# Weight panels beside the inverse and the chunk walk, loaded by transfers of 8 partitions

## What is computed

```python
def step(S, inp):
    r_t, d_t, k_t, v_t, kk_t, b_t = inp
    sa = jnp.einsum('bhvk,bhk->bhv', S, kk_t)
    S = S * d_t[:, :, None, :] - sa[..., None] * b_t[:, :, None, :] + v_t[..., None] * k_t[:, :, None, :]
    y = jnp.einsum('bhvk,bhk->bhv', S, r_t)
    return S, y
...
y = ((y - mean) * lax.rsqrt(var + GN_EPS)).reshape(B, T, D) * gn_w + gn_b
y = (y + bonus.reshape(B, T, D)) * jax.nn.silu(gp)
return y.astype(h.dtype) @ w_out
```

## The kernel before, in words

| panel | slot | what | used up by |
|---|---|---|---|
| 9, 10 | 1, 2 | the two g projections | PE, at about 122 and 145 us |
| 11 to 16 | 3, 0, 1, 2, 3, 0 | gate rows ("ada_rows") 2 to 7 | DVE, four quarters each |
| 17 | 1 | gate panel 8, direct | PE (`ada_direct`, L599), after the walk |
| 18, 19 | 2, 3 | wo_a, both halves | PE, after the walk |
| 20, 21 | 0, 1 | k1, both halves | PE |

## Time and profile before

### The profile page before, as it was taken

How to read it: one execution, slowest core, us unless ns; L and a number is a source line. 1 busy time by engine, 2 the same in 40 slices (tenths; PEclk the granted TensorE clock), 3 DMA queues, 4 the chain that set the end, 5 groups by cost and what they waited for, 6 DMA issues and landing times.

```text
span 1040.6 us, 19605 instructions
## 1 busy us (share of the span) xinstructions
PE 990.0 (95%) x8274; PEld 862.4 (83%) x8274; DVE 745.7 (72%) x1245; ACT 526.0 (51%) x798; POOL 36.5 (4%) x33
## 2 busy tenths in 40 slices
PE   5999999978999999999989999999999899999996
PEld 4888899977788888788857899999698788999995
DVE  5789989577889958646589666666587895664444
ACT  3258431316544686455466445454465855445441
POOL 0000044200000100000000000000000000000000
PEclk9999999989999999999999999999999999999999
DMA  9684410393456560564264478777656444486411
GB/s 366 229 317 162 162 44 4 112 400 143 162 218 232 198 243 26 218 243 162 81 243 162 172 294 291 296 293 266 224 189 230 172 162 162 180 295 253 169 75 41
DMA packets 56263, 205.36 MB, mean 197 GB/s; under 512 B 6376, under 2 KB 6376, under 8 KB 56176
## 3 DMA queue, kind: packets, MB, share of 16 engines
q1 hardware_dynamic: 55584, 202.50, 52.6%
q10 hardware_dynamic: 592, 1.61, 0.5%
HBM read 203.03 MB, written 1.05 MB: 196 GB/s over the span
## 4 chain that ended last, share of the span: by engine, by line
PE 85%; DVE 8%; ACT 3%; DMA 2%; issue 2%; SPq 0%; DVEq 0%; ACTq 0%
PE bank L454 21%; PE bank L455 20%; PE bank L456 20%; PE bank L764 5%; PE bank L403 4%; DVE slot_parts L2027 2%; PE bank L667 1%; DMA ring<-in_stream 1%; PE bank L561 1%; PE bank L906 1%; PE bank L745 1%; PE bank L640 1%; DMA pc<-in_params 1%; PE bank L629 1%; PE bank L536 1%
## 5 line engine op out<-in xcount | busy, mean ns | idle before, releaser
L454 PE MATMUL bank<-page_parts 128*128 128x512 f32 (+3 forms) x1222 | 428.5, 351 | 8.2 <-DVE page_parts L2309 2.1
L2027 DVE TENSOR_TENSOR slot_parts<-ring,page_parts 128x2048 fp32r<-128x2048 f32 (+2 forms) x117 | 261.5, 2252 | 59.4 <-ACT page_parts L1365 59.0
L456 PE MATMUL bank<-page_parts 128*128 128x512 f32 (+2 forms) x750 | 290.7, 388 | 0.0
L455 PE MATMUL bank<-slot_parts,page_parts 128*128 128x512 f32 (+2 forms) x750 | 290.7, 388 | 0.0
L454 PEld LDWEIGHTS bank<-page_parts 128*128 128x128 f32 x1222 | 231.8, 190 | 38.5 <-issue 3.6
L1365 ACT ACTIVATE page_parts<-ring 128x2048 fp32r<-128x2048 f32 (+2 forms) x121 | 224.8, 1883 | 58.0 <-DMA ring<-in_stream 28.0
L456 PEld LDWEIGHTS bank<-page_parts 128*128 128x128 f32 x750 | 141.2, 188 | 29.0
L455 PEld LDWEIGHTS bank<-slot_parts,page_parts 128*128 128x128 f32 x750 | 141.4, 189 | 26.4
L1443 ACT ACTIVATE arena<-bank 128x512 f32<-128x512 f32 (+2 forms) x134 | 74.2, 575 | 128.2 <-PE bank L456 66.9
L455 PE MATMUL bank<-page_parts 128*128 128x256 f32 x472 | 133.6, 283 | 0.0
L456 PE MATMUL bank<-page_parts,slot_parts 128*128 128x256 f32 x472 | 133.6, 283 | 0.0
(11 more groups left out here) (317 smaller groups left out, 1104.6 us busy)
## 6 DMA issues: line engine op xcount, KB each, us to landing
ring<-in_stream SPq DMA_DIRECT2D x380, 512.0 KB, 6.1
arena<-in_x SPq DMA_DIRECT2D x2, 512.0 KB, 4.2
arena<-in_gn ACTq DMA_DIRECT2D x2, 512.0 KB, 4.6
out<-arena SPq DMA_DIRECT2D x2, 512.0 KB, 2.6
cc<-in_consts SPq DMA_DIRECT2D x1, 835.5 KB, 6.5
small<-in_cond ACTq DMA_DIRECT2D x1, 512.0 KB, 7.0
pc<-in_params SPq DMA_DIRECT2D x1, 287.0 KB, 6.9
arena<-in_head_sel ACTq DMA_DIRECT2D x1, 32.0 KB
```

Source lines behind the costliest of these rows:

```text
L454: mm(out, a[0], b[0], start=start, stop=False)
L455: mm(out, a[0], b[1], start=False, stop=False)
L456: return mm(out, a[1], b[0], start=False, stop=stop)
L2027: tt(unit_parts(n)[1], lo, hi, ALU.subtract).then_inc(dv.step("w_lo"), 1)
```

## The change

The nine panels 11 to 19 are loaded in 16 transfers of 8 partitions x 4096 columns instead of 4 transfers of 128 x 1024. What a slot's semaphore must reach is now summed over the panels that went through the slot (`loaded`), 256 for such a panel, 64 for the others. The wait ahead of ("ada_rows", 5) is gone. DVE does four quarters of gate rows at the end of `beside(4)`, and four instead of six before each of the first two copies of S. The waits at lines 384, 592, 1360, 1373 and 1998 all take the new count.

```diff
-PIECES = 4
+PIECES, ROWS = 4, 8
...
+        beside_short_products = [("ada_rows", n) for n in range(2, 8)] + [("ada", 8), ("wo_a", 0), ("wo_a", 1)]
+
+        def narrow(i):
+
+            return order[i][0] in beside_short_products
+
+        def loaded(i):
+
+            return 16 * sum(P // ROWS if narrow(j) else PIECES for j in range(i % SLOTS, i + 1, SLOTS))
...
-                pe.wait_ge(sem(f"slot_loaded{i % SLOTS}"), 16 * PIECES * (i // SLOTS + 1))
+                pe.wait_ge(sem(f"slot_loaded{i % SLOTS}"), loaded(i))
...
                     sp.wait_ge(*order[i - SLOTS][1])
-                if name == ("ada_rows", 5):
-                    sp.wait_ge(*finished(("X", 5, 3)))
+                if narrow(i):
+                    for at in range(0, P, ROWS):
+                        sp.dma_start(ring[at:at + ROWS, i % SLOTS, :], stream[i, at:at + ROWS, :]).then_inc(sem(f"slot_loaded{i % SLOTS}"), 16)
+                    continue
                 for piece in range(PIECES):
...
                     for tb in range(TB):
                         tt(GNT[:, tb, :], GNT[:, tb, :], gn[:, 1, :], ALU.add).then_inc(dv.step(), 1)
                     dve.wait_ge(*dv.last)
+                    ada(4)
...
                 if c < 2:
                     gate_rows(c)
-                    ada(6)
+                    ada(4)
```

More of the change, by code:

```diff
@@ L591, in ada_direct @@
                 b = claim(("ada_row", i))
-                pe.wait_ge(sem(f"slot_loaded{slot % SLOTS}"), 16 * PIECES * (slot // SLOTS + 1))
+                pe.wait_ge(sem(f"slot_loaded{slot % SLOTS}"), loaded(slot))
                 W = ring[:, slot % SLOTS, :].rearrange("p (k n) -> p k n", k=KT)
@@ L1359, in split @@
                     unit = units[n]
-                    act_.wait_ge(sem(f"slot_loaded{unit['slot'] % SLOTS}"), 16 * PIECES * (unit["slot"] // SLOTS + 1))
+                    act_.wait_ge(sem(f"slot_loaded{unit['slot'] % SLOTS}"), loaded(unit["slot"]))
                     if page_used.get(unit["page"]):
@@ L1997, in ada @@
                     if ct == 0:
-                        dve.wait_ge(sem(f"slot_loaded{ada_slots[i] % SLOTS}"), 16 * PIECES * (ada_slots[i] // SLOTS + 1))
+                        dve.wait_ge(sem(f"slot_loaded{ada_slots[i] % SLOTS}"), loaded(ada_slots[i]))
                     W = ring[:, ada_slots[i] % SLOTS, ct * D:(ct + 1) * D]
```

## The result

The changed kernel takes 1070.26 us (median of 4, 1068.21 to 1073.27) against 1042.45 us (1042.16 to 1044.31) for the kernel before, timed beside it: ratio 1.0265 [1.0248, 1.0281]. It is 2.7% slower, and outside the range that was given. The profiled execution took 1071.7 us, its span is 1069.7 us.

The account below looks back on a forecast made before the run. TensorE, with 85% of the chain, was taken as the bound, losing time to late instructions and low clock. Gains 9.2 + 2.5 less 2.2 and 1.0 gave 8.5 us: 1042.3 to 1033.8 us, range 1030 to 1056.

Parts of the forecast that it names:

- rival 2: Panel loads: narrow transfers much slower than 10.1 us a panel; at 20 us, wo_a 18 us late, 1052 us; chance 0.12.
- Part 1: Panels 11 to 19: narrow transfers run on eight engines at 208 GB/s, 10.1 us a panel instead of 5.
- Part 2: Inverse and walk: PE's issue gaps, 8.7 + 0.45 us, and the low clock, 2.5 us, go; together 11.7 us won.
- the gaps: Mostly walk: "issue" pieces where PE waits for nothing named, read as waiting for its instructions; 8.7 + 0.45 us.
- rival 3: Walk and inverse: no difference; gaps stay at half height, new ones in the inverse eat the rest; within 2 us; chance 0.07.
- the clock's 2.5 us: Walk: PE's lower clock follows the gaps at 210 and 216 us and goes with them, winning 2.5 us.
- Part 3: Walk: wide k1 panel makes one or two packets late, 2.2 us; faster PE meets the scan's own chain, 1.0 us.
- Part 4: Inverse: dropping the hold on ("ada_rows", 5) lets panels load from 145 us, at no cost.
- Part 5: Inverse: DVE's four quarters of rows 5, 4.6 us, fit its 5.51 us idle with 0.9 to spare, costing nothing.
- Part 6: After the walk: wo_a0 lands at 213 us and ScalarE takes it at 227; 14 us of slack, no cost.
- Rival 1: Inverse and walk: PE's fetch engine is among the eight, 22 us lost instead of 11.2, 1053 us; chance 0.20.

Follow-up runs that it names:

- e1: The changed kernel, with the 8 rows of each narrow transfer 4 partitions apart instead of neighbouring: 1041.55 us, ratio 0.9968 to the kernel before.
- e7: The changed kernel (8 neighbouring rows), with the first k1 panel loaded by narrow transfers too: 1071.41 us.
- the four patterns above: Rows per transfer and rates: 8 neighbouring, 66 to 70 GB/s; 16 neighbouring, 125 to 135; 8 rows 2 apart, 111 to 132; 8 rows 4 apart, 156 to 225.
- e3: The kernel before with the narrow transfers of 8 neighbouring rows alone; hold and six quarters in the walk kept: 1141.7 us.
- e5: e1 with the first k1 panel loaded by narrow transfers too: 1038.53 us, ratio 0.9958 to the kernel before.
- e13: e5 with panels 14 to 16 in 32 transfers of 4 rows, 8 apart, on four engines: 1037.3 us, ratio 0.9941 to the kernel before.
- e4: The changed kernel with 16 neighbouring rows a transfer, on all sixteen engines: 1115.12 us.
- e11: The changed kernel, with SP issuing each of panels 12 to 20 only when the panel before has landed: 1183.24 us.
- e2: The changed kernel without narrow transfers: all panels wide, no hold, four quarters moved: 1047.34 us, ratio 1.0011 to the kernel before.
- e8: The kernel before with narrow transfers of rows 4 apart, its hold and six quarters kept: 1062.62 us.

## Why the prediction was wrong

The mechanism that decided was rival 2 (chance 0.12), narrow transfers much slower than 10.1 us a panel. It had the direction right, slower, and its price was too low.

1. *Part 1 failed: "eight give 208 GB/s, and a panel of 2.1 MB takes 10.1 us".* The share of engines, one half, was right (0.54). The rate was 66 to 70 GB/s, 30 us a panel, inside the bounds of 10.1 to 64 us but far from the value taken. The reason given for it, that the four pieces of a panel overlap, is true of transfers that write all 128 partitions; it says nothing of eight engines on eight neighbouring rows. The row nearest to the new transfer was head_sel's, and it had been used for the number of engines only, not for a rate. The 208 GB/s is about right for rows 4 apart (156 to 225 in e1).

2. *Rival 2's price failed with it.* It was worked out for T = 20, 1052 us; the panels took about 30 fresh and less in a long load. It looked at wo_a alone. Before that a panel of gate rows was late (9.6 us, the forecast had put nothing there), and in the walk PE stood 11.4 and 8.8 us; but what set the time is wo_a's second half, landed at 282.1 us (e7). The forecast had followed wo_a's first half only. The Trainium skill ("SBUF — State Buffer", Door 1: The DMA port swizzle) says that 8 neighbouring partitions reach two ports; the four patterns above agree with it in order and in ratio. The figure that comes of its table for two, an estimate of about 54 GB/s, is lower than the measured 66 to 70. The time put down to it, over 1130 us, was too high; that estimate left out that the rate climbs in a long load. e3, where the hold kept loads short, has that order of time: 1141.7 us.

3. *Part 2, that the gaps go: half right, seen only where rows are spread.* Beside eight engines the pieces are 0.2 to 2.0 us (e1, e5), not zero; beside four they come to 0.2 us in the inverse (e13). They came in the inverse as well, as rival 3 had it. e5 keeps 4.1 + 1.8 + 0.3 = 6.2 us of pieces against 9.2 before, so 3 us of 9.2 are won, and the clock's 2.5 us are won in full (1.00 from 140 to 236 us). Together that is 5.5 us, of which e5 shows 4.5. That such a piece is PE waiting for its own instructions rests on their spacing, 127 matmuls in e4, and doesn't hold for every one: 6.4 us in the changed kernel and 23.2 in e11 are VectorE's waits. The Trainium skill ("Runtime: NRT & Kernel Launch", Instruction fetch mechanics) has the crossing mostly hidden: without a load the trace agrees (281 matmuls in 8 us in the kernel before), beside a load of eight or sixteen engines it doesn't.

4. *Part 3, k1 wide costs 2.2 us:* e1 and e5 differ in k1 alone. Their direct products are 3.1 us apart (245.72, 242.61), their ratios 0.9968 and 0.9958, whose intervals overlap. The size fits, and isn't shown apart from noise.

5. *Part 4, the hold goes at nothing:* true by itself (e2, 1.0011), but the step looked at its cost only. With 10-us panels keeping it, and the quarters where they were, costs 21 us (e8's span of 1060.3 against 1039.2 in e1).

6. *Part 5, VectorE's quarters hidden:* right. After them it idles for 1.1 us in e1, where the forecast had about 1, and for 3.09 us in the changed kernel, where PE was late itself. The row stands in VectorE's timeline of the changed kernel:

```profile
219.65 0.69 DVE L2271 TENSOR_TENSOR arena<-arena,bank 128x512 f32<-128x512 f32 x1 [3.09 <-PE bank L775]
```

7. *Part 6, 14 us of slack for wo_a:* it hung on part 1. ScalarE waited 14.5 us for the first half. At 10 us a panel it holds (e1).

8. *Rival 1, the fetch engine among the eight, 22 us lost:* pieces do appear in the inverse, which was its sign, but with rows spread they are no longer than beside sixteen engines (2.0 us at most in e1, 2.40 in the earlier trace rows), and their sum in e1 is 3.4 + 2.0 + 1.5 + 0.3 + 0.3 + 0.2 = 7.7 us, not twice the 9.2 of before. Half of it is true, its price isn't.

Open: why an instruction block beside a crowded load is 5 to 11 us late at one time and not late at all at another (e11, 212 to 232 us); and which engines fetch PE's instructions. e13 points to those among the eight that the four-row transfers leave free, or to the smaller share of traffic; no run tells these apart. Open too is whether the crowding sits where the rows are written or where they are read, since every run moved both together.

## What to carry to other kernels

To keep part of the DMA engines free, make a transfer small in rows but spread them: eight rows 4 apart moved 156 to 225 GB/s where eight neighbours started at 66 to 70, with the same share of 0.5 and the same 128 KB. A panel that takes twice as long needs its waits moved too (e8 against e1, 21 us). And look for a late panel first at whoever copies or sums it: PE's own row called the result "issue". Where two things are late side by side, follow the chain before adding them up.

## What the hardware showed that was not expected

- The rate of a crowded load isn't a constant: it climbs from 68 to 215 GB/s in some 90 us of unbroken load, with the share near 0.5 but for the 8 us in which the gn weights load too, and a pause of a few microseconds sets it back to 70 (212:216 in the changed kernel). The GB/s of the changed kernel in 220:228 and in 196:204, each cut into 40 slices:

```profile
GB/s 0 0 82 246 328 0 0 0 0 82 0 0 0 246 164 246 0 0 0 0 0 0 0 82 246 328 82 0 0 0 0 0 0 0 328 246 82 0 0 0
GB/s 0 328 328 0 246 410 0 246 410 0 246 492 0 246 410 0 246 410 0 246 410 0 82 574 0 0 574 82 0 574 82 0 574 82 0 574 82 0 492 164
```

Bytes are counted where a packet ends. The packets end in bursts both times, some 2 us apart at 70 GB/s (32 packets of 16 KB in all) and 0.6 us apart at 215 (104 of them): eight to a burst, as if the eight engines stayed in step and each packet took a third of the time. That they have come to different rows of different transfers by then would fit; no run shows it. With sixteen engines on 16 rows the rate stayed at 125 to 135 GB/s.
- A busy share says nothing of the rate: 1.02 went with 131 GB/s in e4, and 1.03 with 415 in the earlier trace rows.
- A transfer on few partitions delays others too: the gn weights landed 13.5 us after issue beside the crowded panels, and in 4.9 us in e1.
